# Writing two small state outputs straight from the convolution's input buffers, instead of from packed copies

## What is computed

```
def short_conv(h, gate_b, gate_c, w_conv, buf):
    T = h.shape[1]
    full = jnp.concatenate([buf.astype(h.dtype), gate_c * h], axis=1)
    out = w_conv[0] * full[:, 0:T]
    for k in range(1, CONV_WIDTH):
        out = out + w_conv[k] * full[:, k:k + T]
    return gate_b * out, full[:, T:]
```

## Time and profile before

| | before |
|---|---|
| median of three executions | 1541.06 us |
| the profiled execution | 1542.87 us |
| its span in the profile | 1541.1 us |
| mean granted TensorE clock | 0.975 of full speed |
| TensorE matmul busy | 1458.5 us, 95% of the span |
| VectorE, ScalarE, GpSimd busy | 560.4, 467.7, 117.2 us |
| the copies into `ends_p` and `ends_s` | 165 and 221 ns, at 740.0 and 740.1 us |
| the transfers of `ends_p` and `ends_s` | issued at 785.3 and 786.0 us |

### The profile page before, as it was taken

How to read it: one execution, slowest core, us unless ns; L and a number is a source line. 1 busy time by engine, 2 the same in 40 slices (tenths; PEclk the granted TensorE clock), 3 DMA queues, 4 the chain that set the end, 5 groups by cost and what they waited for, 6 DMA issues and landing times.

```text
span 1541.1 us, 27900 instructions
## 1 busy us (share of the span) xinstructions
PE 1458.5 (95%) x11238; PEld 1329.3 (86%) x11238; DVE 560.4 (36%) x1158; ACT 467.7 (30%) x755; POOL 117.2 (8%) x128
## 2 busy tenths in 40 slices
PE   7997999999999996999999989989889999999996
PEld 5676999999999996999999645449789999999995
DVE  0106333333323325335333464645453333232324
ACT  0114333332312114121222345543253334331111
POOL 0402000000001112000000000004320000000110
PEclk9998999999999998999999999999989999999998
DMA  9892444444423232232242423213212222322331
GB/s 345 282 376 93 154 149 151 147 153 145 147 84 95 84 100 56 88 91 72 81 154 103 148 81 88 84 44 122 83 55 83 86 91 82 95 65 84 88 83 66
DMA packets 79188, 180.20 MB, mean 117 GB/s; under 512 B 13861, under 2 KB 39077, under 8 KB 77390
## 3 DMA queue, kind: packets, MB, share of 16 engines
q1 hardware_dynamic: 79118, 179.23, 36.1%
HBM read 173.07 MB, written 10.28 MB: 119 GB/s over the span
## 4 chain that ended last, share of the span: by engine, by line
PE 91%; DVE 4%; ACT 3%; issue 1%; DMA 1%; POOL 0%; SPq 0%; ACTq 0%; DVEq 0%; POOLq 0%
PE PS L1424 72%; PE PS L1347 4%; PE PS L1615 3%; PE PS L1639 3%; PE PS L1445 2%; PE PS L1628 2%; DVE rinv L946 1%; PE PS L1451 1%; PE PS L1328 1%; PE PS L1361 1%; ACT uh L713 1%; PE PS L1397 0%; DMA vec<-in_vec 0%; PE PS L1535 0%; PE PS L1600 0%
## 5 line engine op out<-in xcount | busy, mean ns | idle before, releaser
L1424 PE MATMUL PS<-uh,wh 128*128 128x272 f32 x2032 | 428.3, 292 | 27.1 <-DVE ul L964 26.9
L939 DVE TENSOR_TENSOR wl<-raw,wh 128x1024 fp32r<-128x1024 f32 (+2 forms) x215 | 239.8, 1116 | 576.3 <-ACT wh L688 576.1
L688 ACT ACTIVATE wh<-raw 128x1024 fp32r<-128x1024 f32 (+2 forms) x215 | 203.6, 948 | 805.3 <-PE PS L1424 805.3
L1424 PE MATMUL PS<-uh,wl 128*128 128x272 f32 x2032 | 421.8, 289 | 0.0
L1424 PE MATMUL PS<-ul,wh 128*128 128x272 f32 x2032 | 421.2, 289 | 0.0
L1424 PEld LDWEIGHTS PS<-uh,wh 128*128 128x128 f32 x2032 | 320.0, 190 | 30.2 <-issue 27.4
L1424 PEld LDWEIGHTS PS<-ul,wh 128*128 128x128 f32 x2032 | 321.3, 190 | 0.0
L1424 PEld LDWEIGHTS PS<-uh,wl 128*128 128x128 f32 x2032 | 319.7, 190 | 0.0
L1424 PE MATMUL PS<-hh,wh 128*128 128x272 f32 x704 | 145.7, 288 | 0.9 <-DVE tmp L1013 0.9
L1424 PE MATMUL PS<-hh,wl 128*128 128x272 f32 x704 | 145.7, 288 | 0.0
L1424 PE MATMUL PS<-hl,wh 128*128 128x272 f32 x704 | 145.1, 288 | 0.0
(11 more groups left out here) (226 smaller groups left out, 1285.3 us busy)
## 6 DMA issues: line engine op xcount, KB each, us to landing
raw<-in_w_gu SPq DMA_DIRECT2D x88, 512.0 KB, 3.7
ada_t<-in_w_ada_t SPq DMA_DIRECT2D x44, 512.0 KB, 4.3
raw<-in_w_in SPq DMA_DIRECT2D x39, 512.0 KB, 3.6
ada<-in_w_ada SPq DMA_DIRECT2D x7, 2048.0 KB, 9.9
raw<-in_w_dn SPq DMA_DIRECT2D x32, 384.0 KB, 3.1
raw<-in_w_dn SPq DMA_DIRECT2D x32, 320.0 KB, 2.9
ch<-in_cmp_pages SPq DMA_DIRECT2D x64, 128.0 KB, 4.1
kv<-in_sel_pages SPq DMA_DIRECT2D x128, 64.0 KB, 1.9
```

What stands on the lines that cost most here:

```text
L688: e.activation(wh[:, u % SPLITS, 0:n, :], raw[:, u % RAWS, 0:n, :], ACT.Copy).then_inc(hi_ready, 1)
L939: e.tensor_tensor(wl[:, u % SPLITS, 0:n, :], raw[:, u % RAWS, 0:n, :], f(wh[:, u % SPLITS, 0:n, :]), ALU.subtract).then_inc(lo_ready, 1)
L1424: ins = mm(o[:, a, :], w[:, u % SPLITS, k, :], x[:, k0 + k, HT * a:HT * a + HT], start=(first and k == 0 and w is wh and x is xh), stop=(l ...
```

## The change

The packed buffers, the two copies and their semaphore are gone. SP waits on `psum_free` at the count `O_MGB`, and the two transfers read `fullp` and `fulls` themselves.

```
-        ends_p = sb(ctx, "ends_p", [P, KC, 2])
-        ends_s = sb(ctx, "ends_s", [P, KC, NB, SQ])
...
-        ends_ready = sem("ends_ready")
...
-            e.wait_ge(ends_ready, 1)
-            e.dma_start(d["conv_p"], ends_p[:, :, :]).then_inc(out_done, 16)
-            e.dma_start(d["conv_s"], ends_s[:, :, :, :]).then_inc(out_done, 16)
+            e.wait_ge(psum_free, O_MGB)
+            e.dma_start(d["conv_p"], fullp[:, :, TP:TP + 2]).then_inc(out_done, 16)
+            e.dma_start(d["conv_s"], fulls[:, :, :, 2:2 + SQ]).then_inc(out_done, 16)
...
-            e.tensor_copy(ends_p[:, :, :], fullp[:, :, TP:TP + 2])
-            e.tensor_copy(ends_s[:, :, :, :], fulls[:, :, :, 2:2 + SQ]).then_inc(ends_ready, 1)
```

## The result

The changed kernel takes 1551.7 us (median of four executions, 1551.17 to 1552.94) against 1541.09 us of the kernel before (four, 1540.84 to 1542.87): 10.6 us more, a ratio of 1.007 with a 95% interval of 1.0058 to 1.0082. The profiled execution has a span of 1549.8 us, 8.7 more than before. The forecast of no change was wrong, and the time lies outside its range.

A forecast was written before the change was run, and what follows sets the result against it. The prediction took TensorE to bound the kernel, with 91% of the chain. Its five terms, 0 + 0 + 0 + 0 + 0, gave 1541.0 us against the median of 1541.06, range 1537.0 to 1543.6.

The forecast's parts named there:

- Part 1: The two copies on DVE go: gain 0, hidden by the wait for ACT; at most 0.3 us without that cover.
- Part 2: SP's wait on `psum_free` ahead of the two outputs: already met for 45 us, cost 0.
- Part 3: Outputs in small pieces, 272 more per DMA engine at 27 ns: first `U_MGA` load 7.3 us later, within slack.
- The row's 132 small writes: Smaller packets among 353 while the old outputs drained in 1.4 us: between about 0 and 27 ns each.
- The slack: First `U_MGA` load: landing at 791.25, needed by ACT at 802.85, so 11.6 us, used up at 43 ns a piece.
- The far end of the range of prices: From the `ends_p` transfer alone: 8 pieces an engine in 2.6 us, 325 ns each if none were fixed time.
- rival (b): Small writes delay the first `U_MGA` load and stall TensorE: 1544.1 us at 54 ns, 1545.7 at 60; chance 0.10.
- Part 4: Waits on `out_done`, SP's before `w2p` and DVE's before `chp`: small pieces through by about 795, cost 0.
- DVE's limit of 34 us: Small pieces must last over 34 us, about 118 ns each, to hold up DVE ahead of the `chp` copies.
- Part 5: Everything behind `ends_s` moves down 544 bytes: TensorE's pace in each stage stays as it is, cost 0.
- Rival (a): Moving operand's own address sets TensorE's pace: 1537.6 us (chance 0.10), 1535.4 (0.04) or 1543.2 (0.03).

The follow-up runs named there:

- the early quarters: The changed kernel with both outputs cut into four by channel tile, each quarter issued once its tile is written: 1541.13 us, ratio 0.9992.
- the probe that ends on chip: The kernel before plus one transfer of 4096 pieces of 16 bytes to an on-chip buffer: 1542.38 us, ratio 1.0002.
- the slow probe: The kernel before plus one transfer of 4096 pieces of 16 bytes, side by side in memory: 1548.34 us, ratio 1.0038.

## Why the prediction was wrong, by its steps

**Part 1, the copies: right.** `wl` starts at 739.69 after waiting 1.06 us for ACT, where it had waited 0.85, and the early quarters show no gain without the copies.

**Part 2, the semaphore: right.** SP issues `out_conv_p` 0.05 us after the last key and value output.

**Part 3, the small pieces: the step that failed.** The prediction took "27 ns, because that row is of writes to memory of the same kind, and because 21 ns from the other direction stands close to it". Neither holds. The row's 132 small writes were few, of 32 bytes (122) and 512 bytes (10), and ran between large ones; the reads in runs of 8 bytes end on chip, and the probe that ends on chip has 17 ns. Nor is 27 ns a bound from above, as "at most 27" has it: it is what an assumed rate of the large rows leaves over. At 437 / 16 = 27.3 GB/s, the rate of a window of large reads in the kernel before, the same sum leaves 4.7 us for the 132, 36 ns each (an estimate). The pieces of the change cost 808.3 - 784.1 = 24.2 us for 288, 84 ns each. The rest of the step held. The slack was worked out as 11.6 us and the limit as 43 ns a piece. The load landed 25.3 us after its issue instead of 4.0, so 21.3 us later, which is 78 ns for each of the 272 added pieces. Less the slack that is 9.7 us, and ACT's split came 9.8 us later. One term was off by a factor of three, and it was the one that decided.

That 272 x 0.084 - 11.6 = 11.2 us lies so near the measured loss of 10.6 is in part luck: the 84 ns hold the fixed time of a transfer, which makes the number too high, and the formula leaves out the slow clock after the idle time, which makes it too low.

The error of judgement was in how the bound was closed. The far end of the range of prices was 325 ns and was set aside as fixed time, rightly; but the value taken had no row of many short writes side by side behind it, and the limit stood only 1.6 times above it. With a price open by that much, the chance of 0.10 for rival (b) was far too small, and the range should have reached past 1552. What the prediction quoted of the Trainium skill, "DMA: Bandwidth & Descriptors", section "Specifications", pointed the same way and was set aside by an average over other sizes.

**Part 4, the waits on `out_done`: no cost, as forecast, but not for its reason.** The prediction put the limit at 23.1 us or 80 ns a piece. `out_conv_s` took 23.4 us to land, just past it. SP was not held because the late load had held it first: it waits up to 13.1 us for DVE's splits and comes to `w2p` only at 816.13, after the landing at 808.3. DVE's limit of 34 us was not reached.

**Part 5, the addresses: right.** Every buffer moved, and the pace did not. The splits in FFN2 and in `U_OUT` of the changed kernel, to be held against the earlier trace rows:

```profile
1098.80 1.06 ACT L685 ACTIVATE wh<-raw 128x1024 fp32r<-128x1024 f32 x1 [4.91 <-PE PS L1419]
...
1116.72 1.06 ACT L685 ACTIVATE wh<-raw 128x1024 fp32r<-128x1024 f32 x1 [4.92 <-PE PS L1419]
...
1140.84 1.06 ACT L685 ACTIVATE wh<-raw 128x1024 fp32r<-128x1024 f32 x1 [0.57 <-PE PS L1419]
...
1158.89 1.06 ACT L685 ACTIVATE wh<-raw 128x1024 fp32r<-128x1024 f32 x1 [4.44 <-PE PS L1419]
```

Three units take 17.92 us in `U_OUT` and 18.05 in FFN2, the same as before to 0.01 us. Rival (a) falls. (Its gain was summed as 5.6 us; 6336 x 0.9 ns is 5.7. Nothing hangs on it.) That the two paces come from how the operands lie relative to each other is not shown by this; another cause tied to the stage would look the same.

**Rival (b)** is what happened, at its place and with its releaser; the highest price that it worked out was 60 ns, 1545.7 us. It left out the clock: once TensorE has been idle, it also runs some 20 matmuls at 1.2 GHz, about 2.1 us here.

## What to carry to other kernels

A packing copy on an engine with idle time is cheap (0.4 us here, hidden), and what it buys is long writes to memory; before taking it out, count the pieces that the transfer breaks into and how many of them share 64 bytes (four in the slow probe). A transfer nobody waits for is still in the same queue as the loads behind it: its price is the time by which it delays the next load, less that load's slack, and what the clock takes back after the idle time. If short writes cannot be avoided, cut them up and put them where several microseconds of slack lie behind each part.

## What the runs showed of the hardware that was not expected

- 4096 writes of 16 bytes side by side take 19.3 us to land, 3072 of 64 bytes 4.3 us, by one profile each.
- While short writes drain, a load behind them crawls: in the windows above the engines are 73 to 102% busy from 803 to 809 us and move 31 to 57 GB/s, and the load takes 25.3 us, where it took 4.0 in the kernel before.
- Issuing 4096 pieces held SP for 0.92 us only, and for 0.63 to 1.27 us in the other runs. In these runs the issue time says nothing of the drain.
